# Gated-delta inverses of all chunks ahead of the recurrence, by substitution on VectorE

## The reference, cut to what matters

```python
def gated_delta_chunked(q, k, v, g, beta, s0):
    gc = jnp.cumsum(g.reshape(b, h, n, cs), axis=-1)
    decay = jnp.where(incl, jnp.exp(jnp.where(incl, diff, 0.0)), 0.0)   # diff = gc_i - gc_j
    kb = k * beta[..., None]
    a_mat = jnp.where(strict, jnp.einsum('bhncd,bhnsd->bhncs', kb, k) * decay, 0.0)
    t_mat = lax.linalg.triangular_solve(a_mat + eye, ..., lower=True, unit_diagonal=True)
    u_c = t_mat @ (v * beta[..., None])
    w_c = t_mat @ (kb * jnp.exp(gc)[..., None])
    intra = jnp.where(incl, jnp.einsum('bhncd,bhnsd->bhncs', q, k) * decay, 0.0)
    ...
    def step(s, inp):
        v_new = u_i - w_i @ s
        o_i = qd_i @ s + a_i @ v_new
        s = s * gl_i + kd_i.T @ v_new
```

## Time and profile before

| | |
|---|---|
| Time, median of 3 runs | 2270.39 us (2268.03 to 2272.74) |
| Span of the profiled execution | 2265.7 us, first to last instruction |
| PE busy | 2149.3 us, 95% of the span |
| DVE, ACT, POOL busy | 1163.2, 864.2 and 672.0 us (51%, 38%, 30%) |
| Mean granted TensorE clock | 0.982 of full speed |
| Data moved | 245.27 MB, 108 GB/s over the span |

### The profile page before, as it was taken

The page is one execution under the profiler, slowest core; times in us unless marked ns, Lnnn a source line. Parts: engine busy times, 40 slices in busy tenths (PEclk is TensorE's granted clock), DMA queues, the critical chain, the costliest instruction groups (busy, mean ns, idle before and its releaser), DMA issues.

```text
span 2265.7 us, 35133 instructions
## 1 busy us (share of the span) xinstructions
PE 2149.3 (95%) x12612; PEld 1777.9 (78%) x12612; DVE 1163.2 (51%) x1935; ACT 864.2 (38%) x1673; POOL 672.0 (30%) x607
## 2 busy tenths in 40 slices
PE   7998999999999999999899999898999899998999
PEld 3555888887665888887788888677888778998999
DVE  3745454535458433335543443455555665557665
ACT  2234333232552423233322232354334464454443
POOL 2432222246122111115320122443334643114120
PEclk7999999999999999999999999999999999999999
DMA  7323233332652132322233332220001323554554
GB/s 236 127 68 104 93 113 112 112 95 85 208 184 84 48 102 93 100 95 94 74 97 98 93 102 93 89 75 20 20 20 58 126 90 123 176 176 140 185 177 149
DMA packets 225165, 245.27 MB, mean 108 GB/s; under 512 B 11475, under 2 KB 213652, under 8 KB 224020
## 3 DMA queue, kind: packets, MB, share of 16 engines
q1 hardware_dynamic: 221456, 232.19, 32.3%
q10 hardware_dynamic: 3588, 11.49, 1.4%
HBM read 237.36 MB, written 6.29 MB: 108 GB/s over the span
## 4 chain that ended last, share of the span: by engine, by line
PE 72%; DVE 9%; issue 9%; ACT 4%; POOL 4%; DMA 2%; ACTq 0%; DVEq 0%; POOLq 0%
PE psum L578 51%; PE psum L573 19%; DVE big L2086 5%; PE psum L688 2%; DVE big L2095 2%; POOL whl L1303 1%; ACT big L1517 1%; ACT tmp L1517 1%; POOL big L2805 1%; DMA raw<-in_w_ada_dram 1%; ACT whl L1294 1%; POOL big L2699 1%; ACT big L1520 1%; DMA big<-in_hy_table_dram 0%; POOL big L1393 0%
## 5 line engine op out<-in xcount | busy, mean ns | idle before, releaser
L578 PE MATMUL psum<-hhl,whl 128*128 128x512 f32 (+1 forms) x4416 | 832.4, 348 | 26.4 <-DVE hhl L2216 17.8
L578 PEld LDWEIGHTS psum<-hhl,whl 128*128 128x128 f32 x4416 | 704.6, 193 | 153.0 <-issue 45.0
L1294 ACT CAST whl<-raw 128x512 fp32r<-128x512 f32 x656 | 374.2, 618 | 856.6 <-PE psum L578 851.8
L1303 DVE TENSOR_TENSOR whl<-raw,whl 128x512 fp32r<-128x512 f32 x480 | 330.0, 729 | 487.1 <-ACT whl L1294 486.3
L573 PE MATMUL psum<-big 128*128 128x128 f32 (+6 forms) x2944 | 472.1, 322 | 34.6 <-DVE big L2086 13.7
L578 PE MATMUL psum<-bigr,whl 128*128 128x512 f32 (+1 forms) x2688 | 470.0, 336 | 4.7 <-DVEq L2618 2.5
L578 PEld LDWEIGHTS psum<-bigr,whl 128*128 128x128 f32 x2688 | 414.3, 190 | 57.9 <-issue 4.7
L573 PEld LDWEIGHTS psum<-big 128*128 128x128 f32 (+2 forms) x2944 | 374.1, 193 | 107.9 <-issue 50.6
L1303 POOL TENSOR_TENSOR whl<-raw,whl 128x512 fp32r<-128x512 f32 x176 | 230.0, 1328 | 388.4 <-ACT whl L1294 366.6
L1520 ACT COPY big<-psum 128x512 f32<-128x512 f32 (+2 forms) x324 | 180.0, 556 | 251.3 <-PE psum L573 171.1
L2086 DVE TENSOR_TENSOR big<-big,psum 128x512 f32<-128x512 f32 (+1 forms) x166 | 99.2, 597 | 140.1 <-PE psum L573 136.1
(11 more groups left out here) (153 smaller groups left out, 1458.2 us busy)
## 6 DMA issues: line engine op xcount, KB each, us to landing
raw<-in_w_mlp_dram SPq DMA_DIRECT2D x128, 512.0 KB, 3.6
raw<-in_w_ada_dram SPq DMA_DIRECT2D x96, 512.0 KB, 4.7
raw<-in_w_in_dram SPq DMA_DIRECT2D x88, 512.0 KB, 3.6
raw<-in_w_gate_dram SPq DMA_DIRECT2D x64, 512.0 KB, 3.4
raw<-in_w_branch_dram SPq DMA_DIRECT2D x32, 512.0 KB, 3.4
raw<-in_w_o_dram SPq DMA_DIRECT2D x16, 512.0 KB, 3.4
hy_spectra<-big SPq DMA_DIRECT2D x2, 2560.0 KB, 8.6
big<-hy_spectra ACTq DMA_DIRECT2D x2, 1280.0 KB, 5.8
```

The lines of the kernel that those rows point to most:

```text
L578: m = nc.tensor.matmul(o_, a(p_), b(q_), start=first and i == 0, stop=last and i == 2, skip_group_check=shared)
L1294: nc.scalar.copy(whl[:, r, 0, ks], raw_of(n)[:, ks]).then_inc(S["hi_ready"], 1)
L1303: ins = eng.tensor_tensor(whl[:, r, 1, ks], raw_of(n)[:, ks], whl[:, r, 0, ks].bitcast(F32), ALU.subtract)
```

## The change

The constants with the masks for blocks of 16, 32, 64 and 128 go, and the squaring with them. All 32 matrices of a layer are made and inverted before the first step. DVE and ACT gather their 32x32 diagonal blocks (128 of them) in `diag`; a DVE transposition puts one block on each of the 128 partitions; 30 rounds of two DVE instructions substitute forward in all of them at once (`solved_diagonal`); two more transpositions bring them back. PE then joins 32x32 blocks to 64x64 and 64x64 to 128x128 with small products, whose operands lie in some partitions only (`y_products`, `turned_products`, `plain_products`, `halves`). DVE, ACT and POOL write the results with a minus sign into `dnU`, the turned inverse. The steps keep the products with the state alone.

Other parts follow from it. Key and query products are made once for a tile, no longer for each direction. In the strips the blocks of k come first, then q, then v (`BLK`, `DN_STRIPS`). In layer 0 five `mod` groups run between the `dn` strips, seven around and between the `dz` strips, three between the small products and nine in the steps, with the four `aq` strips. In layer 1 the decays, the keys and most of `A` are made during the `dn` strips, and `dz` and `aq` run while DVE substitutes; nothing fills the steps. The two stores of `hy_spectra` move from SP's queue to ACT's.

```diff
+                def solved_diagonal(between):
+                    dve.wait_ge(S["diag_copied"], 8 * li + 8)
+                    step(V.transpose(solve.rearrange("p r c -> p c r"), diag.rearrange("p g c -> p c g")))
+                    V.memset(solve_flat[:, 0:B * B:B + 1], -1.0)
+                    for j in range(1, B - 1):
+                        n = B - 1 - j
+                        t_ = rstd[:, 256 * (j % 2):256 * (j % 2) + n * j].rearrange("p (r c) -> p r c", r=n)
+                        below = solve[:, j + 1:B, 0:j]
+                        tt(t_, solve[:, j + 1:B, j:j + 1].to_broadcast([P, n, j]),
+                           solve[:, j:j + 1, 0:j].to_broadcast([P, n, j]), MUL)
+                        tt(below, below, t_, SUB)
+                        between(j)
+                    step(V.transpose(inv_n.rearrange("p g c -> p c g"), solve.rearrange("p r c -> p c r")), S["solved"])
+                    step(V.transpose(inv_t.rearrange("p g c -> p c g"), solve), S["solved"])
...
+                def y_products():
+                    pe.wait_ge(S["solved"], 2 * li + 2)
+                    b = fill(("Y64", li))
+                    for st in range(4):
                         for h in range(HEADS):
+                            i = HEADS * st + h
+                            for a in range(2):
+                                for d, hi, lo in pairs(a):
+                                    hs, ls = slice(B * hi, B * hi + B), slice(B * lo, B * lo + B)
+                                    m = mm(b[ls, B * i:B * i + B], dnA_g[hs, 16 * d + i, ls], t_turned_of(d, st, h)[hs, :])
+                    m.then_inc(filled, 1)
...
+                def halves(nm, a, r):
+                    for half in range(2):
+                        b = fill((nm, li, half))
+                        for i in range(8):
+                            for d in range(2):
+                                g = 8 * half + i
+                                m = mm(b[64 * d:64 * d + 64, 64 * i:64 * i + 64], a(d, g), r(d, g))
                         m.then_inc(filled, 1)
...
-                    prod("A2", "Un", "dI", [("blk_ready", 3 * q + 2)])
-                    prod("B2", "dI", "Un", [])
-                    prod("A4", "P2", "P1", [cp("B2")])
...
-                    prod("A8", "P4", "P3", [("U_ready", 6 * q + 1)])
-                    prod("Ub", "P3", "Un", [])
-                    weave(6 * step + 3)
-                    prod("Uc", "P5", "U", [cp("A8"), ("U_ready", 6 * q + 2)])
-                    cur, nxt = "Un", "U"
-                    for lv in range(3):
...
-                            turn(fill((f"V{lv}", q, d)), [hs(s[cur])(h) for h in range(4)]).then_inc(filled, 1)
-                        prod(f"Y{lv}", "dI", cur, [("aoff_ready", 3 * q + lv + 1)])
-                        prod(f"M{lv}", "P2", "P4", [cp(f"V{lv}"), cp(f"Y{lv}")])
...
+                y_products()
+                if li == 0:
+                    query_products(0)
+                    mod_group(1, 12)
+                turned_products()
+                plain_products()
...
+                y_halves()
+                query_products(3 if li else 2)
+                turned_halves()
...
+                new_values(0)
...
+                state_added(0)
+                read_out(0)
...
+                state_read(1)
```

More of the change, by code:

```diff
@@ L290, in build, with reads_out, unit_of, its_before @@
         ROUND = 12582912.0
[L292 to L301, removed]
+        def reads_out(li, m):
+            return li < DEPTH - 1 or m >= 2
+        def unit_of(e):
+            m, d = e // 2, e % 2
+            return 4 * d + MT[d][m]
+        def its_before(li, e):
+            return 8 * li + (e if li < DEPTH - 1 else e - 4)
+        def pairs(a):
+            return [(0, 2 * a + 1, 2 * a), (1, 2 * a, 2 * a + 1)]
         def hn_ready(n, k):
@@ L332, in qk_tile @@
         def qk_tile(li, which, m_):
-            return y[:, ATT, m_ - 2, :] if li and not which else a_qk[:, which, m_, :]
-        def woven(i):
-            return ("aq", i) if i < 4 else ("dz", i - 4)
+            if which:
+                return a_qk[:, 1, m_, :]
+            return y[:, ATT, m_ - 2, :] if li else dnI[:, (0, 1, 4, 5)[m_], :]
         consts_loaded = sem("consts_loaded")
@@ new lines, in y_128, with u_128 @@
+                def y_128():
+                    b = filled_bank(act, ("Y128", li, 1)).rearrange("p (g c) -> p g c", g=8)
+                    step(copy(y128[:, 8:16, :], b), S["y128_act"])
+                    give_fill(act, ("Y128", li, 1))
+                def u_128():
+                    for half in range(2):
+                        b = filled_bank(act, ("M128", li, half)).rearrange("p (g c) -> p g c", g=8)
+                        signals(act, f(dnU_g[64:128, 16 + 8 * half:24 + 8 * half, 0:64], b[64:128], ACT.Identity,
+                                       scale=-1.0), S["u_act"])
@@ new lines, in dn @@
+                solved_diagonal(between)
+                u_diagonal()
+                if li == 0:
+                    mod_cols(1, 10)
+                y_64()
+                if li == 0:
+                    query_matrix(0)
+                    mod_cols(1, 11)
+                u_64()
+                t_64()
+                if li == 0:
+                    query_matrix(1)
+                    mod_cols(1, 12)
+                else:
+                    query_matrix(2)
+                y_128()
@@ new lines, in dn @@
+                query_matrix(3 if li else 2)
+                u_128()
+                if li == 0:
+                    query_matrix(3)
+                    mod_cols(1, 13)
+                    mod_cols(1, 14)
+                states(0)
+                outputs(0)
+                if li == 0:
+                    mod_cols(1, 15)
+                residues(1)
+                read_states(1)
+                if li == 0:
+                    mod_cols(1, 16)
+                states(1)
+                outputs(1)
@@ new lines, in dn @@
+                if li == 0:
+                    mod_cols(1, 17)
+                    mod_cols(1, 18)
+                residues(2)
+                read_states(2)
+                states(2)
+                outputs(2)
+                if li == 0:
+                    mod_cols(1, 19)
+                    mod_cols(1, 20)
+                residues(3)
+                read_states(3)
+                outputs(3)
+                if li == 0:
+                    mod_cols(1, 21)
+                    mod_cols(1, 22)
```

1418 lines of the change are left out of this document (937 added, 481 removed).

## The result

The changed kernel took 2062.71 us (median of 4 runs, 2060.82 to 2063.05), the kernel before beside it 2270.24: ratio 0.9084, interval 0.9071 to 0.9097. The profiled execution has a span of 2061.2 us. In a later series the changed kernel took 2056.24 us (2052.93 to 2061.26, 5 runs) against 2272.31: ratio 0.9041, interval 0.9029 to 0.9054. So its own runs lie up to 10 us apart over the two series, and an edit worth less than 5 us has to be read from rows rather than from medians. The forecast was 2115, so 155 us off the span for the 204.5 that went.

What follows compares the result with a forecast made beforehand. PE, busy 95% of the span, was taken as the bound. Layer 0 -90.6, layer 1 -71.1 and +7 elsewhere gave -154.7: span 2111, median 2115 us. Its own range was 2090 to 2140, for 8 in 10 2060 to 2175.

Steps and rivals of the forecast that it cites:

- the term of the small ones: PE, each layer: 160 products of 32x32 and 64 of 64x64 at 0.125 us each, 28.0 us added.
- the lower bound of 0.06: PE's small products: price in us for one if they overlap better than assumed, 13 us a layer.
- The rule of about 25 ns from start to start: PE's records never start closer, however small the product; so a layer's 448 records cost at least 11 us.
- The remark of the Trainium skill on the tiling mode: Changing the tiling mode drains PE; a few changes a layer move nothing, a drain at each product would be the first rival.
- the first rival: Small products run one after another on PE, 0.56 us each: +195 us, 2310 us, slower; chance 3%.
- the wait ahead of the substitution: Layer 0, after the `dn` strips: substitution starts at about 31 us, PE has 17 us of work, 13.5 idle.
- The substitution: DVE: 60 instructions 22.1 us, three transpositions 3.7, POOL's splits 8 in layer 0; in sum 35 us.
- The waits for weights: `mod` weights in layer 0: 4 us in the sum; PE waiting for `in_w_ada` in its steps would show the forecast wrong.
- the chain of one step: Layer 1's steps: residues, `kv` and the rest add to about 8.5 us a step; 36 us in all, 9.5 idle.
- The fourth rival: More is gained: small products at 0.06 (-29) and half the waits in the steps (-11), 2075 us; chance 20%.
- Second: Substitution not covered: strided operands or shared port double DVE's 26 us, +26 in each layer, 2167 us; chance 17%.
- Third: Clock stays low: small tiles cost twice, +28 in each layer, layer 1's steps +13, 2184 us; chance 10%.

Runs made afterwards that it cites:

- experiment 1: The changed kernel with each group of 32x32 and 64x64 products issued twice, same results: 2082.25 us.
- experiment 6: The changed kernel with POOL's four low-part splits from layer 0's dz strips on cut to 4 of 256 columns: 2052.60 us.
- experiment 2: The changed kernel with small products reordered so that all of one array tile come in a row (`plain_products` unchanged): 2079.41 us.
- experiment 3: The changed kernel with the product of each of the 30 substitution rounds made twice on VectorE: 2076.71 us.
- experiment 4: The changed kernel with layer 1's four `ak` strips moved from behind the steps to the substitution and small products: 2056.39 us.
- experiment 7: The changed kernel with VectorE's first small-product copy ahead of the diagonal's scalings, both layers: 2054.11 us, then 2053.92 beside the changed kernel's 2056.24.

## Why the prediction was right in its direction and too small in its size

**PE's loss.** The work of PE in layer 0's stretch went from 385.1 to 269.5 us, by 115.6 for 101.8 expected; in layer 1 from 267.6 to 158.0, by 109.6 for 98.6. What differs is the term of the small ones. 28.0 us a layer stood there, and the rows of these products are busy 10.6 and 10.8 us in all, 17.4 and 17.2 less. PE's loss does not show 3.6 and 6.2 us of that. The slower clock accounts for at least a part (16 transpositions take 3.21 us at 1452.05 and 1.91 at 1432.15), so the removed products were priced right as far as the rows tell. The nearest row, `csil`, was the wrong neighbour: it streams 256 columns, while a 32x32 product moves 32. Near the lower clock `csil` costs 0.241 us (1.93 / 8), the small product in one tile 0.101, and four tiles by turns bring it to 0.027. With the stops the price was 0.044 to 0.054 us for a product (experiment 1), just under the lower bound of 0.06. The rule of about 25 ns from start to start (the Trainium skill, "TensorE: Matmul & The Clock Gate", "Wait — 56ns, not 53.3ns?") does not hold here for records on different tiles: 13.4 ns with the clock at 0.62 and 10 at the full one, and at the full one even a whole product of two records takes 20. The remark of the Trainium skill on the tiling mode ("TensorEngine Tiling (Array Packing)", "Key Properties") did not lead to the first rival; no run here singles out such a drain.

**Layer 0's waits.** 15.2 us more were expected (11.2, and 4 for weights), and there were 0.6 fewer: 23.9 before, 23.3 after. The idle time from the end of the strips to the small products was 8.7 us for 19.5, and from them to `ak` 10.0 for 8.5. That the wait ahead of the substitution, 13.5 us in the forecast, is so short was not foreseen: PE waits only 4.2 us there, and from 233.35 on it has the `dz` strips. The substitution was priced right as a sum, 35.2 for 35 (its terms add up to 33.8), though two errors cancel: the three transpositions took 6.3 us, 2.1 ns an element and not 1.04, and POOL took 5.7 and not 8 (experiment 6). In the second profile of the same kernel eight rounds met a split instead of six, the substitution took 37.2 us, and PE's wait for it is 5.1 us instead of 1.4; 6 was right as the worse end. The waits for weights did come, which the prediction had named as a sign of being wrong: 5.6 us for `in_w_ada` in this stretch, for 4 in the sum.

**Layer 1's waits.** 18.4 us more, for 27.5 expected. Past the strips it is 17.5 for 22, between the small products 6.1 for 6, in the strips 12.7 for 6 (5.07 for a bank of the decays was not seen). The term that was off most is the chain of one step, 8.5 us. It puts the residues and the `kv` products of both directions one behind the other, as if PE stood meanwhile. In the trace PE starts `vn` of the first direction at 1503.71, 0.05 us after its residues (DVE, 1502.53 to 1503.66), while DVE makes those of the other, and four residues take 1.13 us, not 1.4. The steps took 28.1 us for 36, with 1.2 of wait for 9.5, and PE's rows above have no wait over 0.33 us between them.

**The sum.** Layer 0 -116.2 for -86.6, layer 1 -91.2 for -71.1: together 49.7 us. The start gave 4.9 that nobody had priced, the rest took 4.8 more than the 3 foreseen (among it a POOL wait of 3.98 for 0.40 ahead of `av`, and a clock of 0.98 for 0.99). The fourth rival, "more is gained", is what happened, and beyond its 2075: both of its terms were right in kind. The forecast itself has the mechanism right and two terms too dear, the small products and the steps; that its range still holds the first median, by 2.7 us, is partly luck.

**The others.** First rival: its overlap can be lost (experiment 2), but not in this order of loops. Second: DVE's small instructions did not double; in layer 1 and in layer 0 the substitution is nonetheless at the end of PE's waits (experiment 3), so with DVE's 26 us doubled the loss would have been near what was computed, less what comes back behind it. Third: the clock was low over the small products (0.69 and 0.65, and 0.52 from 1478 to 1492 us), as feared, but at 0.027 us a product that is worth a few us and not 28 a layer. Nor is it shown that small tiles let it fall: it fell behind waits of PE (1.43 and 3.89 us), and with strips in the place of the wait the same 128 records ran at 1.00 (experiment 4). What they did not do is bring it back: in experiment 2 PE was busy 30.4 of the 32.0 us from 1480.1 on, most of it small products, and the clock stood at 0.50.

## What to carry to other kernels

Price a matmul on a small tile by what it streams and by how many different tiles its neighbours use, and write the loops so that neighbours change tiles: here 0.027 us against 0.101 for the same product. Where a recurrence has two independent directions, lay both on the engines' timelines beside each other before you add up the chain of a step. And before you fill a wait of one engine with later work, look at which engine that later work was hiding: here 13 us were won in place and 3 arrived. Four more came when DVE's load behind it had been moved and the orders on ACT and POOL repaired; how much each of these gave was not separated.

## What the runs showed that I had not expected

- Records of 32x32 that go over four tiles by turns start every 10 ns at full clock (128 in 1.29 us) and every 12 to 13 ns near the lower level; over two tiles it is 30 ns there (58 in 1.74 us), in one tile 50.5. For 64x64 at full clock it is 32.5 ns over two tiles by turns against 53 in one (64 records in 3.40 us in experiment 2).
- After some 170 to 220 of these short records PE stands still with no releaser: 3.04 us in layer 0, and 4.78 and 3.39 us in experiment 1, but not where records came at 50 ns. That instructions are not supplied fast enough would fit; no run shows it, and it stays open.
- A DVE transposition of 1024 elements a partition takes 1.91 to 2.25 us, about 2 ns an element, while the small ones of 256 elements on 32 partitions took 0.44 us, near the 0.42 of the formula.
- It is not only POOL's splits that slow DVE: in layer 1 a scaling of 32x512 takes 0.42 us without POOL and 2.00 beside a POOL product on SBUF tiles (L3322). The four took 4.94 us there, and 2.67 in experiment 7, where only the first met it.
- In two executions of one and the same kernel the `dn` strips of layer 0 start 4.9 us apart, by where in the first 40 us the clock stands high; their spans differ by 1.0.
